# Neighbourhood attention: the DRAM writes of the half-word planes are issued by ScalarE behind its copies, not by SyncE between weight loads

## The reference, cut to what matters

```python
proj = h @ w_in
uv, qkv, gates = jnp.split(proj, [2 * GM_WIDTH, 2 * GM_WIDTH + 3 * NA_WIDTH], axis=-1)
...
s = jnp.einsum('bhrcd,bhrikd->bhrcik', qg, k_blk) * scale + bias[None]
p = jax.nn.softmax(s.reshape(b, NA_HEADS, rows, GRID_W, kr * GRID_W), axis=-1)
o = jnp.einsum('bhrcik,bhrikd->bhrcd', p, v_blk)
```

## Time and profile before

| | |
|---|---|
| time, median of 3 | 2322.28 us (2321.55 to 2322.55) |
| profiled execution | 2323.89 us, of which the span of the trace is 2321.4 us |
| PE busy | 2308.1 us, 99% of the span |
| PEld, DVE, ACT, POOL busy | 1935.1, 1499.2, 1285.8, 68.2 us |

### The profile page before, as it was taken

One profiled execution on the slowest core, in us unless ns is written; L12 is line 12 of the kernel. 1 busy time (PEld: TensorE's weight loads), 2 busy tenths in 40 slices (PEclk: granted clock), 3 DMA queues, 4 the chain that ended last, 5 costly groups with the idle time before them and its releaser, 6 DMA issues.

```text
span 2321.4 us, 32543 instructions
## 1 busy us (share of the span) xinstructions
PE 2308.1 (99%) x11879; PEld 1935.1 (83%) x11879; DVE 1499.2 (65%) x2109; ACT 1285.8 (55%) x1969; POOL 68.2 (3%) x94
## 2 busy tenths in 40 slices
PE   9999999999999999999999999999999999999999
PEld 8887778888888888888888888888887888888887
DVE  5656645556577775477776677787877755555554
ACT  5446644444565554355555576657474456666653
POOL 0011100000100000000000000010000000000000
PEclk9999999999999999999999999999999999999999
DMA  8788875776856666566566855554644577877974
GB/s 268 221 254 247 242 234 193 218 223 212 257 182 193 193 184 201 173 209 192 181 187 204 243 159 170 154 172 146 174 149 150 182 221 232 262 216 232 265 222 167
DMA packets 383601, 474.93 MB, mean 205 GB/s; under 512 B 116816, under 2 KB 212976, under 8 KB 383344
## 3 DMA queue, kind: packets, MB, share of 16 engines
q1 hardware_dynamic: 377056, 464.64, 66.5%
q10 hardware_dynamic: 6416, 8.56, 1.2%
HBM read 429.07 MB, written 28.07 MB: 197 GB/s over the span
## 4 chain that ended last, share of the span: by engine, by line
PE 94%; DVE 3%; ACT 1%; DVEq 1%; issue 1%; DMA 0%; ACTq 0%
PE gemm L714 22%; PE gemm L716 22%; PE gemm L715 22%; PE gemm L702 7%; PE aux L702 7%; PE gemm L694 4%; PE aux L694 3%; DVE w_lo L658 1%; PE aux L2261 1%; PE aux L714 1%; PE aux L715 1%; PE aux L716 1%; ACT w_hi L648 1%; PE aux L2473 0%; PE aux L2669 0%
## 5 line engine op out<-in xcount | busy, mean ns | idle before, releaser
L658 DVE TENSOR_TENSOR w_lo<-raw,w_hi 128x1024 fp32r<-128x1024 f32 (+1 forms) x800 | 956.5, 1206 | 589.7 <-ACT w_hi L648 586.3
L648 ACT ACTIVATE w_hi<-raw 128x1024 fp32r<-128x1024 f32 (+1 forms) x800 | 813.5, 1041 | 476.7 <-PE gemm L716 329.1
L714 PE MATMUL gemm<-w_lo,hT 128*128 128x512 f32 x1600 | 634.5, 397 | 6.1 <-DVE w_lo L658 5.8
L716 PE MATMUL gemm<-w_hi,hT 128*128 128x512 f32 x1600 | 624.3, 390 | 0.0
L715 PE MATMUL gemm<-w_hi,hT 128*128 128x512 f32 x1600 | 624.1, 390 | 0.0
L714 PEld LDWEIGHTS gemm<-w_lo,hT 128*128 128x128 f32 x1600 | 301.0, 188 | 73.5 <-DVE w_lo L658 8.8
L716 PEld LDWEIGHTS gemm<-w_hi,hT 128*128 128x128 f32 x1600 | 300.8, 188 | 63.5
L715 PEld LDWEIGHTS gemm<-w_hi,hT 128*128 128x128 f32 x1600 | 301.1, 188 | 59.5 <-issue 0.2
L702 PE MATMUL gemm<-hT,w_hi 128*128 128x512 f32 x704 | 216.8, 392 | 0.0
L702 PE MATMUL aux<-hT,w_hi 128*128 128x512 f32 x672 | 207.6, 390 | 0.0
L714 PE MATMUL gemm<-w_lo,yT_hi 128*128 128x512 f32 x472 | 184.1, 390 | 0.0
(11 more groups left out here) (336 smaller groups left out, 2193.4 us busy)
## 6 DMA issues: line engine op xcount, KB each, us to landing
raw<-in_w_up SPq DMA_DIRECT2D x336, 256.0 KB, 2.9
raw<-in_w_in SPq DMA_DIRECT2D x144, 512.0 KB, 4.7
raw<-in_a_w_in SPq DMA_DIRECT2D x128, 512.0 KB, 3.7
raw<-in_b_w_in SPq DMA_DIRECT2D x128, 512.0 KB, 4.6
raw<-in_w_down SPq DMA_DIRECT2D x76, 512.0 KB, 4.5
raw<-in_w_branch SPq DMA_DIRECT2D x32, 512.0 KB, 5.1
raw<-in_w_out SPq DMA_DIRECT2D x32, 512.0 KB, 4.8
raw<-in_a_w_out SPq DMA_DIRECT2D x32, 512.0 KB, 3.7
```

Of the source, the lines that this page charges most:

```text
L648: nc.scalar.activation(hi, src, ACT.Copy).then_inc(S("hi_done"), 1)
L658: nc.vector.tensor_tensor(lo, src, hi.bitcast(F32), ALU.subtract).then_inc(S("lo_done"), 1)
L714: nc.tensor.matmul(dst, xh, wl[:, k, :], start=h["start"] and k == 0, stop=False)
L716: mm = nc.tensor.matmul(dst, xl, wh[:, k, :], start=False, stop=h["stop"] and k == h["n"] - 1)
```

## The change

The twelve writes of planes of the neighbourhood attention leave SP's program and enter ACT's. Each now stands directly behind the two copies that fill the planes, with a wait of ACT on the semaphore `planes` that those copies count up; for units 2 to 7 the wait for `p_turned` (the DRAM slot has been read) moves to ACT as well. SP keeps the waits for the landed write (`ready`) and the transposing transfers (`behind`) where they were. The other users of `keep_planes` on SP (the merge, the rows of x, the band attention) are unchanged.

```diff
-            def p_keep(u):
-                if u >= 2:
-                    sp.wait_ge(S(f"p_turned{u % 2}"), 16 * (u // 2))
-                keep_planes(na_planes[u % 2], NA_TURNS[u], 3 + u % 2, ("planes_written", "planes_written1")[u % 2])
...
                 if at == 10:
-                    return dict(before={0: lambda: p_keep(0)}, ready={1: lambda: na_wait(even, 3)}, behind={1: lambda: p_spread(0)})
+                    return dict(ready={1: lambda: na_wait(even, 3)}, behind={1: lambda: p_spread(0)})
                 if at == 12:
-                    return dict(before={0: lambda: p_keep(1)}, ready={1: lambda: na_wait(odd, 1)}, behind={1: lambda: p_spread(1)})
+                    return dict(ready={1: lambda: na_wait(odd, 1)}, behind={1: lambda: p_spread(1)})
...
+            def keep_planes(src, i, slot, event):
+
+                act.wait_ge(S("planes"), i + 1)
+                act.dma_start(row_planes[slot].rearrange("(t p) w c -> p t (w c)", p=P),
+                              src[:, :, :, :].rearrange("p t w c -> p t (w c)")).then_inc(S(event), 16)
+
             def rows_apart(name, t, buf, event=None, n=0):
...
                 words_apart(qkv_tok[:, :, :], na_planes[buf], NA_TURNS[name])
+                keep_planes(na_planes[buf], NA_TURNS[name], "qk".index(name[0]), ("planes_written", "planes_written1")[buf])
...
                     words_apart(sc[u % 2][:, :, :], na_planes[u % 2], NA_TURNS[u])
+                    if u >= 2:
+                        act.wait_ge(S(f"p_turned{u % 2}"), 16 * (u // 2))
+                    keep_planes(na_planes[u % 2], NA_TURNS[u], 3 + u % 2, ("planes_written", "planes_written1")[u % 2])
```

More of the change, by code:

```diff
@@ L461, in na_turn @@
                 even, odd = "planes_written", "planes_written1"
-                if at == -8:
-                    return dict(before={0: lambda: keep_planes(na_planes[0], NA_TURNS["q0"], 0)})
                 if at == -6:
                     return dict(ready={0: lambda: na_wait(even, 1)}, behind={0: lambda: turn_planes(qT, 0)})
-                if at == 0:
-                    return dict(before={0: lambda: keep_planes(na_planes[0], NA_TURNS["k0"], 1)})
                 if at == 2:
@@ L470, in na_turn @@
                 if at == 10:
-                    return dict(before={0: lambda: p_keep(0)}, ready={1: lambda: na_wait(even, 3)}, behind={1: lambda: p_spread(0)})
+                    return dict(ready={1: lambda: na_wait(even, 3)}, behind={1: lambda: p_spread(0)})
                 if at == 12:
-                    return dict(before={0: lambda: p_keep(1)}, ready={1: lambda: na_wait(odd, 1)}, behind={1: lambda: p_spread(1)})
-                if at == 16:
-                    return dict(before={0: lambda: p_keep(2)})
+                    return dict(ready={1: lambda: na_wait(odd, 1)}, behind={1: lambda: p_spread(1)})
                 if at == 18:
-                    return dict(before={0: lambda: p_keep(3)}, ready={1: lambda: na_wait(even, 4, 1)}, behind={1: lambda: p_spread(2)})
+                    return dict(ready={1: lambda: na_wait(even, 4, 1)}, behind={1: lambda: p_spread(2)})
                 if at == 20:
-                    return dict(before={0: lambda: keep_planes(na_planes[0], NA_TURNS["q1"], 0)},
-                                ready={1: lambda: na_wait(odd, 2)}, behind={1: lambda: p_spread(3)})
+                    return dict(ready={1: lambda: na_wait(odd, 2)}, behind={1: lambda: p_spread(3)})
                 if at == 22:
                     return dict(ready={1: lambda: na_wait(even, 5)}, behind={1: lambda: turn_planes(qT, 0)})
-                if at == 24:
-                    return dict(before={0: lambda: keep_planes(na_planes[1], NA_TURNS["k1"], 1, odd)})
                 if at == 26:
@@ L487, in na_turn @@
                 if at == 34:
-                    return dict(before={0: lambda: p_keep(4)}, ready={1: lambda: na_wait(even, 6)}, behind={1: lambda: p_spread(4)})
+                    return dict(ready={1: lambda: na_wait(even, 6)}, behind={1: lambda: p_spread(4)})
                 if at == 36:
-                    return dict(before={0: lambda: p_keep(5)}, ready={1: lambda: na_wait(odd, 4)}, behind={1: lambda: p_spread(5)})
-                if at == 40:
-                    return dict(before={0: lambda: p_keep(6)})
+                    return dict(ready={1: lambda: na_wait(odd, 4)}, behind={1: lambda: p_spread(5)})
                 if at == 42:
-                    return dict(before={0: lambda: p_keep(7)}, ready={1: lambda: na_wait(even, 7, 3)}, behind={1: lambda: p_spread(6)})
+                    return dict(ready={1: lambda: na_wait(even, 7, 3)}, behind={1: lambda: p_spread(6)})
                 if at == 44:
```

## The result

The changed kernel took 2327.59 us at the median of 20 runs (2325.29 to 2328.88), the kernel before 2323.05 us in its 20 runs beside them (2321.55 to 2324.78). The ratio is 1.0019, with a 95% interval of 1.0012 to 1.0025. The loss is real and small: 0.19%, just under the 0.2% that the forecast took for the least that can be told from no change, and the interval leaves no change out. The profiled execution took 2326.65 us.

What follows compares the result with a forecast made beforehand. Softmax handed between VectorE and ScalarE was taken to bound the stretch where TensorE waits. Exposed issues of 2.99 us plus 0.5 of clock, total 3.5, on a median of 2322.28 gave 2325.8 us, range 2323.0 to 2334.5.

Steps and rivals of the forecast that it cites:

- The bound: Around the neighbourhood attention, softmax passed between VectorE and ScalarE bounds two stretches; TensorE waits 5.8 us, always for the low split.
- the chains: VectorE-ScalarE sequences behind TensorE's two stall clusters, units 0 and 1 on the first, 4 and 5 on the second: 1.24 us each.
- unit 2's place: ScalarE's issue behind unit 2's copies, one of seven where TensorE does not wait: only shortens a lead, taken as 0.
- SyncE's side: Twelve issues leave SyncE, 6.7 us out of slot waiting; waits for landed writes, 15.8 us, shrink; gain for TensorE 0.
- The rival on the faster side: Earlier landed writes let weight loads at the head of the chains start earlier: at most 7.5 us gained, 2314.8; chance 0.06.
- The price of a place: One exposed issue behind ScalarE's copies costs 0.22 us plus 0.40 us duration: 0.62 us, ends 0.6 and 0.83.
- The sum: Exposed issues at units 0 and 1, 4 and 5, and 6: 1.24 + 1.24 + 0.51 = 2.99 us.
- The clock: Behind the first stall, grown from 2.01 to 3.25 us, a longer 1.2 GHz stretch: 0.5 us, between 0 and 1.7.
- its own sign of being wrong: Prediction wrong if TensorE waits for anything but the low split, the clock drops in the second cluster, or the chains break.
- Being held behind transposes: ScalarE's issues at units 1 and 5 wait 3.77 and 2.77 us for SyncE's transposes: 2332.3 to 2334.0; chance 0.30.
- the rule of the Trainium skill: One shared descriptor generator is locked until an instruction's descriptors exist, and profiled time includes that wait; ScalarE's issues would wait behind transposes.
- A free issue: ScalarE's sequencer starts the issue while the copies still run, so it costs nothing: 2322.3; chance 0.08.

Runs made afterwards that it cites:

- the first experiment: Against the kernel before, ScalarE issues only seven writes (q and k of both groups, units 2, 3, 7), SyncE the other five: 2323.97 us, ratio 1.0006.
- the repeated run: The changed kernel unedited, timed and profiled once more beside the kernel before: 2327.15 us, ratio 1.0018.
- the shift with ScalarE's writes: The changed kernel with ScalarE's copies of the eight units, and the writes right behind them, one weight half later: 2320.33 us, ratio 0.9992.
- the shift with covered issues: The changed kernel with the units' copies one step later and ScalarE's writes one further step later, behind a weight half: 2319.30 us, ratio 0.9985.
- only the five places: Against the kernel before, ScalarE issues only the writes of units 0, 1, 4, 5 and 6, SyncE the others: 2327.41 us, ratio 1.0018.
- late issue: The changed kernel with each write issued one step later, behind the copy of the next weight half: 2323.46 us, ratio 1.0002.
- second issue: The changed kernel with a second, small 64 KB transfer issued by ScalarE right behind each of the twelve writes: 2331.25 us, ratio 1.0034.

## Why the prediction was right, point by point

**The bound.** That the handing to and fro between VectorE and ScalarE bounds two stretches is shown three ways: five issues on the chains cost about as much as all twelve, seven off them 0.9 us, which is not clear of nothing, and moving the copies by one step gained 4.5 us. That only delays on the chains count is not quite so: unit 2's place, taken as free, has a stall of its own where the clock is granted in full, 0.5 us with one issue (211.78 in the first experiment, 212.80 in the repeated run) and 1.0 with two. The forecast had read the slack of that place from a profile in which TensorE ran through a slow stretch there.

**SyncE's side, taken as 0.** The rival on the faster side did not come. But the reasoning failed in two places. The waits for landed writes were to shrink from 15.8 us and were 16.5. And the term was not 0: it had nothing for the transposes, which stay on SyncE and are issued while writes now run from another queue. The twelve transposes of this part took 48.2 us to issue in the kernel before (summed over its L422 rows from 142.87 to 303.8 us). In all four profiles in which SyncE writes the sum is 48.2 to 49.6 us, in all six in which ScalarE writes all twelve it is 52.5 to 55.4. Four of them stand close together between about 218 and 253 us, and the last brings the k of the second group. In the repeated run of the changed kernel:

```profile
221.69 5.96 SPq L422 DMA_TRANSPOSE pT<-row_planes_kept  x1
...
229.54 5.49 SPq L422 DMA_TRANSPOSE pT<-row_planes_kept  x1
...
236.94 6.38 SPq L422 DMA_TRANSPOSE qT<-row_planes_kept  x1
...
248.30 4.98 SPq L422 DMA_TRANSPOSE kT<-row_planes_kept  x1
```

Before, the last of these was issued at 244.94 and TensorE just did not wait. TensorE waited for that k in four of the six profiles with all twelve writes on ScalarE (0.7 to 1.9 us), for 0.9 us in the one with seven and 0.2 us in the one with five, and in none of the four with SyncE's. Weight loads stand behind the same transposes on SyncE, and they come late too: between 215 and 262 us TensorE also waited for splits of late halves, 0.5 us in the repeated profile, 2.2 us in the shift with ScalarE's writes and 1.7 us in the shift with covered issues. Turned tiles and splits together, it waited there 0.7 to 3.0 us in five of the six profiles with twelve writes on ScalarE (not in the first of the changed kernel), and not at all in the four with SyncE's. That the second queue's traffic is what lengthens the transposes is inferred from this grouping; no run isolated it.

**The price of a place.** Forecast 0.62 us with 0.60 and 0.83 as ends; 0.59 and 0.67 us measured at units 0 and 1. The issue itself took 0.38 us at the median (forecast 0.40), the wait for the copies 0.12 alone.

**The sum.** Forecast 2.99 us, all on the chains. The waits for the split grew by 2.2 us in the first profile and 3.3 in the second, but waits mix with the clock and with late loads. A cleaner reading is the start of the same low split of VectorE in each kernel, ahead of and behind each chain (start us; in brackets by how much the stretch since the mark before is longer than in the kernel before):

| kernel | ahead of the first chain | behind it | ahead of the second | behind it |
|---|---|---|---|---|
| before | 184.83 | 203.57 | 262.95 | 306.49 |
| changed | 184.92 | 204.49 (+0.83) | 263.82 (-0.05) | 309.25 (+1.89) |
| changed, repeated | 185.73 | 205.30 (+0.83) | 266.64 (+1.96) | 312.31 (+2.13) |
| only the five places | 185.14 | 205.08 (+1.20) | 263.24 (-1.22) | 308.65 (+1.87) |
| late issue | 184.84 | 203.59 (+0.01) | 262.20 (-0.77) | 305.52 (-0.22) |
| second issue | 185.02 | 206.07 (+2.31) | 267.06 (+1.61) | 314.04 (+3.44) |

The chains grew by 0.83 + 1.89 = 2.7 us and 0.83 + 2.13 = 3.0 us in the changed kernel, and by 3.1 us with the five places alone: the forecast of 2.99 is borne out. The first chain had 1.24 us forecast and grew by 0.83, since VectorE's scaling of unit 1 took 1.37 us instead of 1.85 in both profiles and hid half a microsecond; in the run with five places it grew by 1.20. What the sum lacked lies between the chains: unit 2's place and SyncE's side. There the kernel before and the first profile of the changed one have a slow stretch of the clock and the other rows have none, so the other rows' numbers hold that gain, too. It is about 1.5 us, as the late issue shows, whose stretch is 0.77 us shorter although TensorE waits 0.7 us for k in it.

**The clock.** The 0.5 us taken for a longer slow stretch was not seen: granted 0.83 over 205 to 215 us in the first profile, as before, and 1.00 in the second. The timed executions say the same. A profile with a slow stretch has a mean granted clock of 0.999 and one without 1.000; 0.999 or less was recorded in 12 of the changed kernel's 31 executions and in 35 of the 81 of the kernel before that ran beside the experiments. Among those at 1.000 alone the medians are 2327.10 and 2327.16 us in the two measurements of the changed kernel, against 2322.67, 2322.45 and 2322.68 before, so the loss is 4.4 to 4.7 us with the clock granted in full. The loss does not come from the clock.

**The number.** The median moved by 4.5 us where 3.5 was forecast, 3.0 for the chains and 0.5 for the clock. The chains cost what was forecast and the clock nothing; that its 0.5 us stood in for part of what was missing elsewhere is luck. Two terms taken as 0 were mis-sized: unit 2's place, worth 0.5 us where the clock is granted in full, and SyncE's side, where TensorE waited 0 us in the first profile and 1.5 + 0.5 + 0.2 = 2.2 us in the second. That these two make up the whole remainder is not shown: the kernel with only the five places loses 4.4 us at the median too, and its one profile has 0.2 us of such waiting and no stall at unit 2's place. The forecast of 2325.8 us for the median also started from 2322.28, the median of three runs, where twenty gave 2323.05. By its own sign of being wrong, that TensorE waits for anything but the low split, the prediction held in the first profile and failed in the second.

**The rivals.** Being held behind transposes is refuted by the issue at 193.47 and by the one of unit 5, which took 0.44 us beside a transpose. By the rule of the Trainium skill ("Perfetto Trace Analysis", on DMA instructions of the hardware descriptor path), that issue should have waited for the lock until the transpose's descriptors were done. If these take most of the transpose's 5.91 us, the trace does not agree, for the issue started 0.49 us into it and took 0.45; no row shows when the descriptors were done. A free issue is refuted where ScalarE waits for its own copy; where a weight half stands between, the loss was 0.4 us, not clear of nothing.

## What to carry to other kernels

A transfer's issue can be moved to the engine that makes the data, but if it stands directly behind the producer, the engine waits for its own work and issues with nothing running: here 0.6 us each time. One instruction later, with something else already in the engine, no cost could be measured. Before moving any wait, ask which engine's chain is the bound at each place. Seven delays off it cost too little here to be told from nothing by the times, and the larger prize may be the order of what stands on it. Slack read from a profile with a slow stretch of the clock may be gone in the next execution. And ask what stays behind: the transposes left on SyncE took longer, and the loads and tiles behind them came late.

## What the runs showed that was not expected

ScalarE's issues beside a transpose of SyncE pass it: 0.44 to 0.45 us at units 1 and 5 against a median of 0.38. Writes on a queue of their own did not land sooner: 4.0, 6.4 and 11.6 us (least, median, most) in the changed kernel and 3.5, 5.4 and 10.9 in the kernel before, and the twelve transposes beside them took 53.2 us to issue instead of 48.2.
